# S5 branch of a hybrid decoder step: block matrices kept without their zeros, u laid out by pair parity, small matmuls placed on four or eight parts of the PE array, and the scanned state laid out with its steps side by side

## The reference

```python
bu_re = einsum('blgc,gnc->blgn', ug, bbar_re)      # 128 groups g of 16 channels c, 64 states n
bu_im = einsum('blgc,gnc->blgn', ug, bbar_im)
# complex diagonal scan over l:  s[l] = a * s[l-1] + bu[l]
y = einsum('blgn,gcn->blgc', s_re, c_re) - einsum('blgn,gcn->blgc', s_im, c_im)
y = y.reshape(bsz, L, S5_WIDTH) + d_skip * u
v = gelu(y) @ w_glu
```

## Time and profile before

| | |
|---|---|
| Median of 3 runs | 2540.27 us (2537.93 to 2541.57) |
| The profiled execution, its own time | 2539.22 us |
| Its span, first to last instruction | 2537.3 us |
| PE busy | 2503.7 us (99%) |
| DVE busy | 1667.7 us (66%) |
| ACT busy | 1123.8 us (44%) |
| Mean granted TensorE clock | 0.993 |

### The profile page before, as it was taken

The page is one execution under the profiler, slowest core; times in us unless marked ns, Lnnn a source line. Parts: engine busy times, 40 slices in busy tenths (PEclk is TensorE's granted clock), DMA queues, the critical chain, the costliest instruction groups (busy, mean ns, idle before and its releaser), DMA issues.

```text
span 2537.3 us, 53388 instructions
## 1 busy us (share of the span) xinstructions
PE 2503.7 (99%) x19651; PEld 2457.7 (97%) x19651; DVE 1667.7 (66%) x3139; ACT 1123.8 (44%) x1779; POOL 19.8 (1%) x41
## 2 busy tenths in 40 slices
PE   9999999999999998999999999999999999999998
PEld 8999999999999998999999999989999999999998
DVE  6787878777787867679885665565555555544444
ACT  6454544545454444554354333453333333333332
POOL 1000000000000001000000000000000000000000
PEclk9999999999999999999999999989999999999999
DMA  7566665657666679445467677545555555565453
GB/s 198 175 194 193 205 194 171 200 165 212 181 203 193 182 202 232 111 123 159 145 180 204 198 199 221 158 146 164 163 165 163 165 164 165 165 209 160 158 161 125
DMA packets 656221, 448.66 MB, mean 177 GB/s; under 512 B 71192, under 2 KB 645928, under 8 KB 654912
## 3 DMA queue, kind: packets, MB, share of 16 engines
q1 hardware_dynamic: 639104, 433.72, 58.7%
q10 hardware_dynamic: 16928, 12.51, 1.6%
HBM read 409.35 MB, written 36.76 MB: 176 GB/s over the span
## 4 chain that ended last, share of the span: by engine, by line
PE 93%; DVE 3%; ACT 1%; DMA 1%; issue 1%; SPq 0%; ACTq 0%; POOL 0%; DVEq 0%; POOLq 0%
PE acc L2070 28%; PE acc L2071 27%; PE acc L2072 27%; PE side L2057 3%; PE side L2402 1%; DVE w_lo L1330 1%; PE side L2161 1%; PE side L2245 1%; PE side L2233 1%; PE side L2437 1%; PE side L2438 1%; ACT w_hi L816 1%; PE side L2422 1%; PE side L2080 0%; DMA raw<-in_w_in_dram 0%
## 5 line engine op out<-in xcount | busy, mean ns | idle before, releaser
L1330 DVE TENSOR_TENSOR w_lo<-raw,w_hi 128x1024 fp32r<-128x1024 f32 (+2 forms) x692 | 830.6, 1208 | 644.8 <-ACT w_hi L816 640.9
L816 ACT ACTIVATE w_hi<-raw 128x1024 fp32r<-128x1024 f32 (+2 forms) x692 | 717.0, 1045 | 1006.3 <-PE acc L2072 958.0
L2070 PE MATMUL acc<-h_hi,w_hi 128*128 128x288 f32 x3472 | 1043.0, 300 | 1.9 <-DVE w_lo L1330 1.9
L2072 PE MATMUL acc<-h_hi,w_lo 128*128 128x288 f32 x3472 | 1024.3, 295 | 0.0
L2071 PE MATMUL acc<-h_lo,w_hi 128*128 128x288 f32 x3472 | 1023.3, 295 | 0.0
L2070 PEld LDWEIGHTS acc<-h_hi,w_hi 128*128 128x128 f32 x3472 | 653.7, 188 | 6.4 <-issue 3.3
L2071 PEld LDWEIGHTS acc<-h_lo,w_hi 128*128 128x128 f32 x3472 | 653.2, 188 | 2.8
L2072 PEld LDWEIGHTS acc<-h_hi,w_lo 128*128 128x128 f32 x3472 | 652.4, 188 | 0.0
L2070 PE MATMUL acc<-f_hi,w_hi 128*128 128x288 f32 x704 | 208.4, 296 | 0.0
L2072 PE MATMUL acc<-f_hi,w_lo 128*128 128x288 f32 x704 | 207.7, 295 | 0.0
L2071 PE MATMUL acc<-f_lo,w_hi 128*128 128x288 f32 x704 | 207.5, 295 | 0.0
(11 more groups left out here) (376 smaller groups left out, 2865.5 us busy)
## 6 DMA issues: line engine op xcount, KB each, us to landing
raw<-in_w_in_dram SPq DMA_DIRECT2D x512, 256.0 KB, 3.3
raw<-in_w_ffn_up_dram SPq DMA_DIRECT2D x352, 256.0 KB, 3.4
raw<-in_w_ffn_down_dram SPq DMA_DIRECT2D x160, 256.0 KB, 3.0
raw<-in_w_ssm_out_dram SPq DMA_DIRECT2D x128, 256.0 KB, 4.0
raw<-in_w_glu_dram SPq DMA_DIRECT2D x128, 256.0 KB, 3.6
h<-in_state_ssm_dram SPq DMA_DIRECT2D x64, 256.0 KB, 4.7
out_ssm_sample_dram<-h SPq DMA_DIRECT2D x64, 256.0 KB, 3.3
raw<-in_w_out_dram SPq DMA_DIRECT2D x64, 256.0 KB, 3.3
```

What stands on the lines that cost most here:

```text
L816: copy = lambda out, in_, **k: nc.scalar.activation(out, in_, ACT.Copy, **k)
L1330: tt(w_lo[:, slot, 0:n], raw[:, slot, 0:n], w_hi[:, slot, 0:n].bitcast(F32), ALU.subtract).then_inc(lo_ready, 1)
L2070: mm(o_, wh, xh[:, kt, :], start=first and i == 0, stop=False)
L2072: done = mm(o_, wl, xh[:, kt, :], start=False, stop=last and i == n - 1)
```

## The change

What it does:
- The block matrices `qc`, `qc2` and `tbd` are [128, 2, 8, 64], without the zeros; DVE writes a part with one operation over 128 partitions instead of two over 64. GpSimd's zero fills go.
- u and y are laid in `u2` by the parity e of the pair: partitions 64e to 64e + 63 hold one group, the free index the pair and the half g2. A quarter of u or y takes 16 transfers instead of 8.
- `q_turn` does two pairs at once (8 transposes a block instead of 16), both parts in one quarter. `responses` are on eight parts of the array (64 rows x 32 columns), `inputs` and `s5_out` on four (64 x 64), `t_products` on two at a time (rows and columns 64e). `inputs` are in two quarters (three of four double pairs, then one), `s5_out` and `t_products` in one.
- `p_copy` makes two copies a block instead of four, `inputs_copy` eight instead of twelve, `t_block` four instead of eight.
- `st5` becomes [128, 2, 64 pairs, 72 steps]: the 72 steps of a pair are adjacent, and one step of all pairs is 2 x 64 numbers, 72 apart.
- DVE copies the responses before it makes matrices, where it did so after.

The diff, cut to its core:

```diff
-    qbd, at = sb("qbd", [P, 2, PB, P], F32, at)
+    qc, at = sb("qc", [P, 2, PB, 64], F32, at)
...
-    st5, at = sb("st5", [P, 72, 2, PAIRS], F32, top // 32 * 32 - 72 * 2 * PAIRS * 4)
+    st5, at = sb("st5", [P, 2, PAIRS, 72], F32, top // 32 * 32 - 72 * 2 * PAIRS * 4)
...
+        def front(i):
+            return (s2, s3) if i % 2 == 0 else (s0, s1)
+        def back(i):
+            return front(i + 1)
...
-            for g2 in range(2): for j in range(4):
-                act.dma_start(dst, u2[r:r + 16, q * n:(q + 1) * n, :]).then_inc(sem("y5_stored"), 16)
+            for e in range(2): for j in range(4):
+                for g2 in range(2):
+                    act.dma_start(dst[g2], src[:, g2]).then_inc(sem("y5_stored"), 16)
...
-                for g2 in range(2):
-                    r = slice(64 * g2, 64 * g2 + 64)
-                    dst = bd[r, part, :, 64 * g2:64 * g2 + 64].rearrange("x p (j c) -> x p j c", j=DL)
-                    last = tt(dst, v[0][r], v[1][r], op)
+                dst = bd[:, part, :, :].rearrange("x p (j c) -> x p j c", j=DL)
+                tt(dst, v[0], v[1], op).then_inc(sem(s + "_matrices"), 1)
...
-            col = lambda n: st5[:, n, :, :]
+            col = lambda n: st5[:, :, :, n]
...
+            def q_turn(i):
+                pe.wait_ge(sem("q_matrices"), i * 2 + 2)
+                wait(pe, "p_copied", i * 4 - 2)
+                for k in range(2):
+                    for r in range(4):
+                        last = turn(front(i)[k][:, r * P:(r + 1) * P], (qc, qc2)[i % 2][:, k, 2 * r:2 * r + 2, :].rearrange("p e m -> p (e m)"))
+                    last.then_inc(sem("q_turned"), 1)
...
+                pe.wait_ge(sem("p_ready"), i * 2 + 2)          # responses
+                for k in range(2):
+                    for r in range(4):
+                        for g2 in range(2):
+                            last = mm(front(i)[g2][32 * r:32 * r + 32, 0:P], ct5[rows, k, pair:pair + 2, :], q[rows, k, 2 * r:2 * r + 2, :], start=k == 0, stop=k == 1)
...
+                for r in range(3) if part == 0 else (3,):       # inputs
+                    for k in range(2):
+                        for e in range(2):
+                            bank = back(i)[e] if part == 0 else front(i)[1 - e]
+                            for g2 in range(2):
+                                last = mm(bank[cols, at_:at_ + NK], pw5[rows, k, r, cols], u2[rows, i * PB + 2 * r + g2, :], **one)
...
+                for r in range(4):                              # s5_out
+                    for k in range(2):
+                        for e in range(2):
+                            for g2 in range(2):
+                                last = mm(banks[g2][64 * e:64 * e + 64, r * NK:(r + 1) * NK], q[rows, k, 2 * r + e, :],
+                                          st5[rows, k, i * PB + 2 * r + e, :], start=k == 0, stop=k == 1)
...
+                    if z % 2 == 0 and kt == 0:
+                        q_turn(i)
+                    if z % 2 == 0 and kt == 2:
+                        responses(i)
+                    if z % 2 == 1 and kt == 1:
+                        responses_turn(i)
+                        inputs(i, 0)
+                    if z % 2 == 1 and kt == 3:
+                        inputs(i, 1)
```

More of the change, by code:

```diff
@@ L1070, in p_copy, with inputs_copy @@
                 act.wait_ge(sem("q_turned"), i * 2 + (k + 1))
[L1071 to L1078, removed]
+                wait(act, "p_product", i * 2)
+                copy(pw5[:, k, :, :], front(i)[k][:, :].rearrange("p (r m) -> p r m", m=P)).then_inc(sem("p_ready"), 1)
+            def inputs_copy(i, part):
+                act.wait_ge(sem("p_product"), i * 2 + (part + 1))
+                if i == 0 and part == 0:
                     act.wait_ge(sem("y_summed"), 3 * NG)
                     groups_stored(act)
[L1081 to L1086, removed]
+                r0, n = (0, 3) if part == 0 else (3, 1)
+                block = slice(i * PB, i * PB + PB)
+                states = st5[:, :, block, 1:64].rearrange("p c (r e) k -> p e c r k", e=2)
+                ends = en5[:, :, :, block].rearrange("p k c (r e) -> p e c r k", e=2)
+                for e in range(2):
+                    src = (back(i)[e] if part == 0 else front(i)[1 - e])[:, 0:2 * n * NK].rearrange("p (r c k) -> p c r k", c=2, k=NK)
+                    copy(states[:, e, :, r0:r0 + n, :], src[:, :, :, 0:63])
+                    copy(ends[:, e, :, r0:r0 + n, :], src[:, :, :, 63:72]).then_inc(sem("p_copied"), 1)
             def t_block(i):
@@ L1091, in t_block @@
                 if i == 0:
[L1092 removed]
+                    act.wait_ge(sem("p_product"), 16)
                 wait(act, "t_product", i * 2 - 2)
[L1094 to L1098 removed]
+                for j in range(DL):
+                    src = gs5[:, i * PB:i * PB + PB, :] if j == 3 else                         (s2, s3)[i % 2][:, (2 - j) * P:(3 - j) * P].rearrange("p (g c) -> p g c", c=S5C)
+                    last = copy(tbd[:, i % 2, :, 16 * j:16 * j + 16], src)
                 last.then_inc(sem("tbd_ready"), 1)
@@ L1169, in _ @@
                     else:
-                        for m in range(4):
-                            inputs_copy(i, m)
+                        inputs_copy(i, 0)
+                        inputs_copy(i, 1)
                 if T0 <= z < T0 + 24:
@@ L1760, in q_matrices @@
                 if i < 2 and part == 0:
-                    dve.wait_ge(sem("s5_zeros"), 2 + i)
+                    dve.wait_ge(*reach(("ya_front", "ya_stored")[i], 16 * 4))
                 wait(dve, "r_product", i - 1)
-                matrices(i, part, (qbd, qbd2)[i % 2], bb5, pq5, ALU.subtract, ALU.add, "q")
+                matrices(i, part, (qc, qc2)[i % 2], bb5, pq5, ALU.subtract, ALU.add, "q")
             def o_matrices(i, part):
@@ L1801, in skip_added @@
                 if k == 0:
[L1802 to L1805, removed]
+                    dve.wait_ge(*reach("skip_landed", 64))
+                    for e in range(2):
+                        r = slice(64 * e, 64 * e + 64)
+                        last = tt(dd5[r], dd5[r], bc(ident[r, 64 * e + 48:64 * e + 64], PAIRS, 1), ALU.mult)
                     last.then_inc(sem("skip_masked"), 1)
@@ L1812, in _ @@
             a4i9, a4r9 = bc(po5[:, 1, 3, :], 9, 1), bc(po5[:, 0, 3, :], 9, 1)
-            sre, sim = st5[:, 63:72, 0, :], st5[:, 63:72, 1, :]
+            sre, sim = [st5[:, k, :, 63:72].rearrange("p g k -> p k g") for k in range(2)]
             def finals(part):
@@ L1864, in _ @@
                     gs_copy(i)
+                if 0 <= i < 8 and part == 0:
+                    responses_copy(i)
                 if 0 <= i + 1 < 8:
@@ L1868, in _ @@
                     o_matrices(0, part)
-                if 0 <= i < 8 and part == 0:
-                    responses_copy(i)
                 if z in (T0 - 4, T0 - 2):
@@ new lines, in t_products, with s5_out @@
+                wait(pe, "t_copied", i * 2)
+                for h in range(2):
+                    for p in range(4 * h, 4 * h + 4):
+                        for e in range(2):
+                            rows = slice(64 * e, 64 * e + 64)
+                            last = mm((s0, s1)[h][rows, (p % 4) * NK:(p % 4 + 1) * NK], tbd[rows, i % 2, p, :], u2[rows, i * PB + p, :], **one)
+                    last.then_inc(sem("t_product"), 1)
+            def s5_out(i):
+                q, banks = (qc, qc2)[i % 2], ((s0, s1), (s2, s3))[i % 2]
+                if i == 0:
+                    pe.wait_ge(sem("scan_stepped"), 63)
+                    pe.wait_ge(*reach("t_copied", 16))
+                pe.wait_ge(*reach("o_matrices", i * 2 + 2))
+                wait(pe, "s5_y_copied", i * 2 - 2)
+                for r in range(4):
+                    for k in range(2):
+                        for e in range(2):
+                            for g2 in range(2):
+                                rows = slice(64 * g2, 64 * g2 + 64)
+                                last = mm(banks[g2][64 * e:64 * e + 64, r * NK:(r + 1) * NK], q[rows, k, 2 * r + e, :],
+                                          st5[rows, k, i * PB + 2 * r + e, :], start=k == 0, stop=k == 1)
+                                if r == 3 and k == 1 and e == 1:
+                                    last.then_inc(sem("y5_product"), 1)
```

160 lines of the change are left out of this document (62 added, 98 removed).

## The result

The changed kernel takes 2544.20 us (median of 20 runs, 2539.14 to 2549.87), the kernel before 2539.36 (20 runs, 2534.70 to 2541.61): ratio 1.0022, 95% interval 1.0015 to 1.0028. It is slower by a little: some 5 us, clear of noise. The measured time lies inside the forecast range (2520 to 2551), but the outcome that the prediction held likeliest, no change, was the wrong one; its own sum had 1.8 us more.

What follows compares the result with a forecast made beforehand. PE was taken to set the input stage and DVE nearly the scan; ACT and DVE alternate in the tail. The sum 2539.2 - 23.9 + 17.0 + 8.7 = 2541.0 us became a forecast of 2540, range 2520 to 2551.

Steps and rivals of the forecast that it cites:

- no change: Whole kernel: time within 0.2%, some 5 us, of the kernel before; chance 0.34, range 2535 to 2545.
- what block 6 gives back: Input stage: PE comes sooner and waits for both ACT copies behind the first gate; 1.5 us lost.
- Input stage, -23.9: Slots z = 12 to 27: packed small matmuls save PE 25.4 us over eight blocks, less 1.5 in block 6.
- rival C: Input stage and outputs: 64-row parts don't run side by side, 0.112 us a group; 2547 us, chance 0.13.
- E: Rival, input stage: copies bound it, so packing does nothing for the span; 2555 us or more, chance 0.04.
- Scan, +17.0: Slots z = 28 to 58: DVE's strided state columns delay the last scan step by 17.0 us.
- price of 0.33 a step: DVE in the scan: 384 strided numbers a step at 0.86 ns each, 0.33 us.
- Rival A: DVE in the scan: strided columns cost nothing, 2516 us, or half, 2530; chance 0.27.
- Tail, +8.7: Outputs to z = 74: cheaper matrices, but more ACT stores and strided final states; ends 8.7 us later.
- the walk: Tail: slots followed from the scan's end with estimated durations, giving PE's waits and an end 8.7 us later.
- Rival B: Tail: shorter stores are cheap to issue, 0.34 us each, losing 10 us less; 2530 us, chance 0.11.
- Rival D: DVE in the scan: the strided write is charged too, 0.44 us a step; 2550 us, chance 0.11.

Runs made afterwards that it cites:

- steps apart: Changed kernel with st5's old layout again, one step of all pairs as 128 adjacent numbers: 2517.10 us, ratio 0.9919 to the kernel before.
- stores on GpSimd: Changed kernel with all four y_store calls issued by GpSimd instead of ACT, still 16 transfers a quarter: 2516.73 us, ratio 0.9918 to the kernel before.
- eight stores: Changed kernel with a quarter of y stored by 8 transfers instead of 16, same bytes: 2525.60 us, ratio 0.9955 to the kernel before.
- Moving the gate: Changed kernel with GpSimd stores and paired steps, first gate placed behind slot z = 24's two copies on ACT: 2493.02 us, ratio 0.9826 to the kernel before.
- in pairs: Changed kernel with GpSimd stores, two steps side by side and the pairs of steps apart: 2493.38 us, ratio 0.9818 to the kernel before.

## Why the prediction was right and wrong

- **What failed, in short.** "No change" failed because two terms were too small: what block 6 gives back in the input stage (1.5 taken, 2.8 measured, since the clock fell behind a wait for which no such loss was charged) and the stores in the tail (+16.0 taken, +18.5 measured). And the sum itself had 1.8 us more, of which the forecast kept 0.6.
- **Input stage, -23.9: measured -21.9.** Slots are 4.95 and 5.01 us; the terms gave 4.90 and 5.01. The 64 output instructions on 64x64 parts take 1.23 us with going in and out, 0.077 a group of four, so rival C (0.09 and more a group) falls, and E with it. Of the 2.0 missing, 0.4 are the even slots and 0.3 is z = 12, for which the prediction had no term (0.7 over the later slots, 0.4 in the kernel before). The step that failed is "block 6 gives back 1.5". It gave back 2.8: ACT had the table load and the gates ahead of both copies,

```profile
1067.42 1.28 ACT L1071 ACT_TABLE_LOAD   x1
1068.71 0.71 ACT L1071 ACTIVATE gth<-acc 128x288 f32<-128x288 f32 x2
1069.45 0.36 ACTq L1073 DMA_DIRECT2D mix_scratch<-gth  x1
1069.91 1.08 ACT L825 ACTIVATE pw<-side 128x512 f32<-128x512 f32 x2 [0.49 <-ACT gth L1071]
```

  PE waited 1.81, and lost 1.3 more in z = 25, where the granted clock was 0.57 over 4 us:

```profile
1072.00:1076.00 4.00, 4.00 (x23) 3.82 (x21) 3.43 (x6) 1.06 (x1) 0.00 (x0) 0.57 0.22 82
```

  The prediction had charged the clock only behind waits over 3.5 us. But the same wait did not always cost it: with steps apart and with stores on GpSimd, where that part of the program is the same, PE waits 1.8 us at the same place,

```profile
1068.00:1072.00 4.00, 4.00 (x73) 3.76 (x72) 3.91 (x8) 1.57 (x2) 0.00 (x0) 1.00 0.22 81
```

  the clock stays at 1.00 (this row is from steps apart), and z = 24 and 25 take 6.8 and 5.0 us (7.1 and 6.3 in the changed kernel), which is 1.2 given back, less than the 1.5. With eight stores it fell again (0.66 over the same 4 us, 7.5 and 5.9). So the wait was priced well, and the other 1.5 us is a fall of the clock that some executions had and others not; the prediction had put it at nothing. Moving the gate took the wait away, and with it that chance.
- **Scan, +17.0: measured +16.1** (the first output matmul is 1227.11 - 1089.06 = 138.1 us after the stage's start; 121.9 before). The price of 0.33 a step was taken from one row of another operation; the runs show 0.114 (L1797) + 0.133 (L1805) + 2 x 0.053 (L1798, L1799) = 0.353, over 0.292 and 0.219 in the kernel before. Rival A falls. As the price was 0.02 too low and the stage still came out 0.9 shorter than forecast, another term of that sum is some 2 us too large; no run shows which.
- **Tail, +8.7: measured +11.8** (1323.47 - 1227.11 = 96.4, where it was 1316.69 - 1232.1 = 84.6). The waits came where the walk had them (2.0, 6.0, 11.4 and 1.3 us at z = 61, 64, 73 and 74, where it had 2.1, 4.9, 12 and 3). The term that was mis-sized is the stores: 0.50 each was taken, the four bursts took 9.13 + 8.53 + 9.05 + 8.71 = 35.4, 0.55 each, where the kernel before took 16.9 for its 32. That is +18.5 for +16.0, or 2.5 of the 3.1 missing. The rest can be the clock: the chunk of z = 73 runs at half of it,

```profile
1313.00:1318.00 5.00, 4.66 (x19) 4.66 (x20) 4.90 (x9) 3.07 (x8) 0.00 (x0) 0.50 0.66 193
```

  and takes 1320.17 - 1313.35 - 1.29 = 5.53 us for 3.19, so 2.3 lost where 1.6 was charged. No run tells the two shares apart. Rival B falls. Why 0.55 stays open: in the kernel before with 16 stores, bursts of as many rows took 7.6 to 7.9 us, with the same median of 0.46 for one, but the longest was 0.75 there and 1.90 here.
- **Sum.** 2.0 and 3.1 too little, 0.9 too much: +5.9 in the stretch where +1.8 was forecast. The 0.9 that the scan had too much hid a part of the other two. The forecast then went from 2541.0 down to 2540 because the walk comes out 1 to 2 us late on the known kernel; but +8.7 is the difference of two walks, from which such an error drops out, so that step had no ground. Rival D at 0.44 a step is 6.8 us by the prediction's own numbers, 2547 and not 2550; nothing hangs on it.
- **The bound of 5 us for "no change" was too wide.** It was read from the spread of three runs; twenty of each tell 0.07%.

## What to carry to other kernels

Before a fast engine is made faster, list what each slower engine's program does in the same stretch: here the packing was worth 41 us in the stretch, and all of it went to a layout that DVE paid for and to DMA issues that stood in ACT's program. A layout that two engines read at right angles has a middle: with two of the numbers of one side adjacent, DVE paid nothing and PE a fifth of what it paid at full distance. And a repair is priced with its cover: moving the stores was worth 2 us before the change and 27 after it.

## What was not expected of the hardware

- Distance 2 is as fast as distance 1 for a DVE operand of 128 f32 (292 ns both), distance 24 (469) slower than 16 (378) and 72 (391).
- PE's moving side has a price for distance too: 64 instructions of 72 columns on four parts take 1.23 us adjacent, 1.54 in pairs, 2.83 at 128 numbers apart.
- A plain store issued by GpSimd takes it 0.53 us in the median, ACT 0.46; but ACT's longest were 1.90, so a burst of 16 took 8.3 to 8.5 us on GpSimd and 8.5 to 9.1 on ACT.
- The granted clock is no fixed price of a wait. Behind the wait of 1.8 us in z = 24 it was 0.57 over 4 us in the changed kernel and 1.00 in two experiments with the same program there; it also stayed at 1.00 around the 1.9 us in front of z = 74 in the kernel before. What decides it was not tried.
